# A hybrid attention block on one core: group B by chunks of 64 queries, and the input projection in three turns

## The reference, cut to what matters

```python
proj = x @ w_in                      # 2048 tokens, 1024 -> 2756 columns
qa, ka, va, ga, qi, ki, wi, qb, kb, vb, gb = split(proj)
# group A: 8 heads, one key/value head
score = sum_h wi[h] * relu(qi[h] @ ki.T)          # 4 index heads
idx   = top_k(score where chunk(key) <= chunk(query), 256)
ya    = softmax(qa @ ka[idx].T / 8 - slope * |t - idx|) @ va[idx]
# group B: 8 heads, 2 key/value heads; a chunk of 64 queries
# sees the 64 keys before it and its own 64 keys
yb    = softmax([qb @ kb.T / 8 - slope * dist, sink])[..., :-1] @ vb
y     = concat(ya * silu(ga), yb * silu(gb)) @ w_out
out   = layer_norm(2**0.25 * x + y)
```

## Time and profile before

| | us |
|---|---|
| median of 3 runs (1501.98 to 1502.45) | 1502.32 |
| span of the profiled execution, first to last instruction | 1501.2 |
| PE busy | 1395.7 (93%) |
| DVE busy | 1164.6 (78%) |
| ACT busy | 969.1 (65%) |
| POOL busy | 491.5 (33%) |
| projection, first to last matmul of L1314 | 11.5 to 578 |
| last stage, from its first matmul | from 1316.6 |

### The profile page before, as it was taken

How to read it: one execution, slowest core, us unless ns; L and a number is a source line. 1 busy time by engine, 2 the same in 40 slices (tenths; PEclk the granted TensorE clock), 3 DMA queues, 4 the chain that set the end, 5 groups by cost and what they waited for, 6 DMA issues and landing times. The chain is left out here.

```text
span 1501.2 us, 19745 instructions
## 1 busy us (share of the span) xinstructions
PE 1395.7 (93%) x6551; PEld 1038.2 (69%) x6604; DVE 1164.6 (78%) x2406; ACT 969.1 (65%) x1879; POOL 491.5 (33%) x310
## 2 busy tenths in 40 slices
PE   6998999899999896799899899999998999999997
PEld 5887877678788675556466566566665776578886
DVE  3377879868999888689989998989987756347765
ACT  3385876874789258988549789569997767711010
POOL 1332132651523343412411212112214745423332
PEclk9999999999999997899999999999999999999999
DMA  6322131532222336422211323103214222124442
GB/s 247 98 74 103 57 112 68 165 103 70 90 79 67 129 86 166 98 72 68 72 43 56 77 50 91 55 14 86 67 49 132 85 58 80 43 92 158 150 135 90
DMA packets 104534, 136.42 MB, mean 91 GB/s; under 512 B 6611, under 2 KB 81367, under 8 KB 104175
## 3 DMA queue, kind: packets, MB, share of 16 engines
q1 hardware_dynamic: 91280, 92.73, 22.6%
q10 hardware_dynamic: 9504, 31.66, 5.3%
q0 software_dynamic: 3648, 10.76, 2.3%
HBM read 92.73 MB, written 42.34 MB: 90 GB/s over the span
## 5 line engine op out<-in xcount | busy, mean ns | idle before, releaser
L1612 DVE TENSOR_SCALAR_CACHE_REDUCE above<-dist,trial 128x512 bf16<-128x512 int32 (+13 forms) x224 | 345.5, 1543 | 5.8
L1139 ACT ACTIVATE above<-dist,trial 128x384 bf16<-128x384 int32 (+13 forms) x224 | 280.7, 1253 | 21.5 <-DVE trial L1585 11.7
L1314 PE MATMUL psum<-x_hi,w_hi 128*128 128x512 f32 x640 | 254.6, 398 | 33.3 <-POOL w_lo L941 13.5
L1314 PE MATMUL psum<-x_lo,w_hi 128*128 128x512 f32 x640 | 252.5, 394 | 0.0
L1314 PE MATMUL psum<-x_hi,w_lo 128*128 128x512 f32 x640 | 252.1, 394 | 0.0
L1248 ACT ACTIVATE prob<-psum 128x512 f32<-128x512 f32 x272 | 159.0, 592 | 116.8 <-PE psum L1462 59.0
L1712 DVE CUSTOM_DVE_ANT_0 junk<-psum,mask 128x512 bf16<-128x512 f32 (+3 forms) x320 | 183.1, 605 | 38.9 <-PE psum L1385 19.5
L1462 PE MATMUL psum<-prob,vw 128*65 128x512 f32 x376 | 184.1, 592 | 0.1
L1449 PE MATMUL psum<-qa_mix,ka_mix 128*128 128x512 f32 x272 | 161.5, 594 | 6.3 <-DMA qa_ext<-minus_max 6.1
L1314 PEld LDWEIGHTS psum<-x_hi,w_hi 128*128 128x128 f32 x640 | 122.3, 191 | 62.9 <-POOL w_lo L941 15.7
L933 POOL CAST w_hi<-raw 128x1024 fp32r<-128x1024 f32 x40 | 52.0, 1299 | 286.5 <-PE psum L1314 279.7
(11 more groups left out here) (160 smaller groups left out, 3001.1 us busy)
## 6 DMA issues: line engine op xcount, KB each, us to landing
raw<-w_tiles SPq DMA_DIRECT2D x40, 512.0 KB, 3.8
proj<-staged ACTq DMA_DIRECT2D x40, 512.0 KB, 3.1
qb_raw<-proj SPq DMA_DIRECT2D x32, 256.0 KB, 4.0
qa_raw<-proj SPq DMA_DIRECT2D x32, 256.0 KB, 4.5
yt_raw<-y_t SPq DMA_DIRECT2D x16, 512.0 KB, 5.2
x_row<-x_res SPq DMA_DIRECT2D x16, 512.0 KB, 3.9
out<-z ACTq DMA_DIRECT2D x16, 512.0 KB, 2.6
x_raw<-xT SPq DMA_DIRECT2D x12, 512.0 KB, 4.2
```

The lines of the kernel that those rows point to most:

```text
L1139: nc.scalar.activation(above[:, 0, 0:n], src, ACT.Sign, scale=-1.0, bias=u, accum_out=count[:, 0:1]).then_inc(sign_counted, 1)
L1314: last = pe.matmul(psum[:, 2 * u + m, :], wt[:, u, k, :], xt[:, k, 512 * m:512 * m + 512], start=(k == 0 and q == 0), stop=(k == KT - 1 an ...
L1612: v.tensor_scalar(above[:, 1, 0:n], src, u, None, ALU.is_ge, ALU.add, accum_out=count[:, 1:2]).then_inc(own_counted, 1)
```

## The change

Group B takes chunks of 64 queries: a stationary operand of 128 columns is 64 queries of two heads, the moving operand the 128 keys that this chunk sees. Rows of `lb` are then 128 keys and one sink; no key is masked away. The probabilities are divided by their sum on POOL before they are transposed (`level_b`, new), 8 transposes are enough, and `mix_b` has the values as the stationary operand and 256 columns of probabilities as the moving one, four times. Its result has the rows that the output wants, so `y_b` and `columns_b` are gone. The columns of `w_in` and the rows of `w_out` of group B are permuted on the host for it, and `shift_values` copies the values once, shifted by 64 tokens, into `vs`.

The projection has three turns: tiles 0 to 2 of the first half, all 20 of the second, then tiles 3 to 19 of the first. The first half's x is loaded, rounded and split a second time for the third turn. The splits of the second turn are DVE's (`OWN_SPLITS`), those of the third POOL's. The 16 `norm` steps are bound to the first two turns, and `dots` of steps 1 to 5 stand in the list of the second.

The planner breaks ties in a fixed way, some assumed durations are larger (a search step 0.1 on DVE and 0.08 on ACT), and the table `PREFER` is new throughout.

```diff
+PASSES = [(0, range(0, KEY_TILES - 1)), (1, range(0, N_TILES)), (0, range(KEY_TILES - 1, N_TILES))]
+SEQUENCE = [(half, t) for half, some in PASSES for t in some]
+PLACE = {tile: n for n, tile in enumerate(SEQUENCE)}
+OWN_SPLITS = 2 * KT + 2
...
-            add("DVE", 0.6 + n / 960, "search", p, i, needs=[("begin" if i < 16 else "turn", p), ("search", p, i - 1)])
-            add("ACT", 1.0 + (n - P) * 0.00083, "sign", p, i,
+            add("DVE", 0.7 + n / 960, "search", p, i, needs=[("begin" if i < 16 else "turn", p), ("search", p, i - 1)])
+            add("ACT", 1.08 + (n - P) * 0.00083, "sign", p, i,
...
+        if t == PASSES[turn][1][-1] and turn < 2 and k == 0:
+            needs += [("product", *tiles[n - 1], KT - 1)] + [("norm", b) for b in NORM_ORDER[8 * turn:8 * turn + 8]]
...
-        for p in ((1, 2, 3), (4, 5))[half]:
+        for p in ((), (1, 2, 3, 4, 5), ())[turn]:
             dots_of(p, None)
...
-        add("DVE", 0.2, "den_b", b, needs=[("exp_b", b, H - 1), ("y_b", b - 1)])
+        add("DVE", 0.2, "den_b", b, needs=[("exp_b", b, H - 1), ("level_b", b - 1)])
+        add("POOL", 2.6, "level_b", b, needs=[("den_b", b)])
...
+            def shift_values():
+                sp.wait_ge(tile_mm, 2 * N_TILES)
+                sp.wait_ge(norm_out, NB)
+                sp.dma_start(vs[0:HD, 1:NB, :], vw[HD:P, 0:NB - 1, HD + 1:HD + 1 + P]).then_inc(values_shifted, 16)
+                sp.dma_start(vs[HD:P, :, :], vw[0:HD, :, HD + 1:HD + 1 + P]).then_inc(values_shifted, 16)
...
+            def level_b(b):
+                pool.wait_ge(b_rec, b + 1)
+                settled()
+                nc.gpsimd.tensor_tensor(lb[:, :, 0:P], lb[:, :, 0:P], rec_b[:, :].unsqueeze(2).broadcast_to([P, H, P]),
+                                        ALU.mult).then_inc(b_level, 1)
...
-                pe.wait_ge(b_exp, 2 * b + g + 1)
+                pe.wait_ge(b_level, b + 1)
                 banks_free(2)
-                for i in range(4):
-                    last = pe.transpose(psum[:, 2, P * i:P * i + P], lb[:, 4 * g + i, P:2 * P], ident[:, :])
-                    if b:
-                        last = pe.transpose(psum[:, 3, P * i:P * i + P], lb[:, 4 * g + i, 0:P], ident[:, :])
+                for i in range(H):
+                    last = pe.transpose(psum[:, 2 + i // 4, P * (i % 4):P * (i % 4) + P], lb[:, i, 0:P], ident[:, :])
...
-                for h in range(H):
-                    o = psum[:, 2, HD * h:HD * h + HD]
-                    v0 = HD + 1 + HD * (h // 4)
-                    qs = slice(P * (h % 4), P * (h % 4) + P)
-                    if b:
-                        pe.matmul(o, ptb[:, h // 4, 1, qs], vw[:, BLOCKS[b] - 1, v0:v0 + HD], start=True, stop=False)
-                    last = pe.matmul(o, ptb[:, h // 4, 0, qs], vw[:, BLOCKS[b], v0:v0 + HD], start=(b == 0), stop=True)
+                for g in range(2):
+                    for c in range(2):
+                        keys = vw[:, BLOCKS[b], HD + 1:HD + 1 + P] if c else vs[:, BLOCKS[b], :]
+                        last = pe.matmul(psum[:, 2 + g, 2 * P * c:2 * P * c + 2 * P], keys, ptb[:, g, 2 * P * c:2 * P * c + 2 * P],
+                                         start=True, stop=True)
```

More of the change, by code:

```diff
@@ L84 @@
           "search": ("sortable", "begin", "search", "sign", "turn", "limits", "equal", "above", "masks"),
-          "band": ("load_qb", "round_qb", "split_qb", "window", "bias_b", "max_b", "exp_b", "put_sink", "den_b", "turn_b",
-                   "copy_b", "mix_b", "y_b", "columns_b", "gate_b"),
+          "band": ("load_qb", "round_qb", "split_qb", "window", "bias_b", "max_b", "exp_b", "put_sink", "den_b", "level_b", "turn_b",
+                   "copy_b", "mix_b", "gate_b"),
           "scan": ("load_qa", "round_qa", "split_qa", "positions", "scan", "scan_max", "top_of_chunks", "turn_max", "leave_max", "place_max"),
@@ L141, in timed @@
                 by_engine.setdefault(self.engine[piece], []).append((piece, time))
-            for engine, some in by_engine.items():
+            for engine in ("SP", "POOL", "DVE", "ACT", "PE"):
+                some = by_engine.get(engine, [])
                 now = free.get(engine, 0.0)
@@ L178, in timed, with whole_plan @@
         return start
-def whole_plan(final=True):
+def whole_plan():
     plan = Plan()
     add = plan.add
-    tiles = [(half, t) for half in range(2) for t in range(N_TILES)]
-    x_of = lambda half, k: k + half * (KT + 2)
+    tiles = SEQUENCE
+    x_of = lambda turn, k: k + (KT * turn + 2 if turn else 0)
+    split_kind = lambda m: "split_x" if m < OWN_SPLITS else "split_x2"
     def dots_of(p, bank_lock):
@@ L285, in whole_plan @@
         for k in range(KT):
-            for t in range(2):
-                products(half, t, k)
-        for t in range(2, N_TILES):
+            for t in some[0:2]:
+                products(turn, half, t, k)
+        for t in some[2:]:
             tile(half, t)
-            if (half, t) == (0, N_TILES - 1):
-                for b in NORM_ORDER[0:8]:
+            if t == some[-1] and turn < 2:
+                for b in NORM_ORDER[8 * turn:8 * turn + 8]:
                     norm(b)
             for k in range(KT):
-                products(half, t, k)
@@ L295, in whole_plan @@
-        if half:
-            for b in NORM_ORDER[8:]:
-                norm(b)
-        for p in ((1, 2, 3), (4, 5))[half]:
+                products(turn, half, t, k)
+        for p in ((), (1, 2, 3, 4, 5), ())[turn]:
             dots_of(p, None)
-    end = ("product", 1, N_TILES - 1, KT - 1)
+    end = ("product", *tiles[-1], KT - 1)
     for i in range(2):
-        add("POOL", 1.0, "keys_rest", i, needs=[("norm", NORM_ORDER[-1]), ("split_x2", 2 * KT + 1), ("round_keys", 1)])
+        add("POOL", 1.0, "keys_rest", i, needs=[("norm", NORM_ORDER[-1]), ("round_keys", 0), ("round_keys", 1)])
@@ L1303, in product @@
             def product(half, t, k):
-                g, u = half * N_TILES + t, t % 2
+                g = PLACE[half, t]
+                u = g % 2
+                turn = [turn for turn, (of, some) in enumerate(PASSES) if of == half and t in some][0]
                 if k == 0:
```

338 lines of the change are left out of this document (170 added, 168 removed).

## The result

The changed kernel takes **1513.05 us** (median of 4 runs, 1511.44 to 1513.54) where the kernel before takes 1502.31 beside it: a ratio of 1.0066, 95% interval 1.0053 to 1.0078. It is slower by 0.7%, where I had forecast 1443 and a range of 1410 to 1478.

The account below looks back on a forecast made before the run. PE, busy 93%, was taken as the bound on average, sharing 612 to 900 us with DVE. 1501.2 - 47 (group B) - 12 (order) = 1442 us span; the runs' median lies 1.1 us higher, so 1443, range 1410 to 1478.

Parts of the forecast that it names:

- Group B on PE: Narrower products and fewer transposes in group B's blocks save 3.1 us a block, 47 us of PE's time in all.
- My mark, PE's busy time: Sign set beforehand: PE's busy time should be about 47 us less, plus what the clock gives.
- I count no change of PE's losses there: Attention, 612 to 900 us: the new order's extra DVE work stands against 14 us saved on DVE, so 0.
- a microsecond counts in full from 900 us on: Attention after 900 us: PE idles little, so each microsecond taken from its work shortens the span by as much.
- My own sign: Forecast wrong if PE's idle time from the projection's end to 900 us grows by more than 10 us.
- The order: Projection: the new list wins back 12 of PE's 29 us idle; bounds 29 us won and 10 us lost.
- The third turn: Projection: extra loads, roundings and splits of x cost PE 0, bounded by 3 us; 13 us more before the search.
- The second account, by DVE: Whole kernel counted by DVE's work: last masks at 1177 us, then the work behind them, giving 1470 us.
- DVE is the bound: Rival: the last two blocks wait for the last mask, 1470 us; chance 0.28 shared with the lost half.
- Group B's time is off the path: Rival: only about half of 47 us comes and the order brings nothing, 1477 us; chance within the shared 0.28.
- The chain through POOL stalls PE: Rival: `level_b` waits in POOL's queue and holds up `turn_b` on PE, 1506 us; chance 0.05.
- The contention rule: POOL beside two-SBUF-input DVE instructions may take 6.53 us, not 2.40; for `level_b` in the attention 2.49 was kept.

Follow-up runs that it names:

- before_less_b: The kernel before, order untouched, with half of group B's transposes and mix products left out: 1491.22 us, ratio 0.9921.
- apart: The changed kernel with the planner's list taking one whole weight tile after the other, not alternating between two: 1502.59 us, ratio 0.9994.
- before_tuned: The kernel before with one whole weight tile after the other and a new planner table `PREFER`: 1511.94 us, ratio 1.0070.

## Why the prediction was wrong, step by step

- **Group B on PE, 47 us: right.** The ledger shows 47.2 us less work, the four products start 0.43 us apart, no transpose of an output follows them. My mark, PE's busy time, was a poor one: it fell by 23 us, because the slow clock stretches it.
- **"I count no change of PE's losses there": the step that failed.** I took PE's saved time in the attention off the span one for one, and held the losses of 600 to 900 us for DVE's. `before_less_b` shows the price in the old order: 0.36 us for each microsecond of group B taken away, against 0.86 for each added to the changed kernel. My sentence that a microsecond counts in full from 900 us on came from PE's small idle time there. That idle time was small while the narrow matmuls were there: with half of them left out it went from 11.8 to 23.0 us from 900 us on. By this price the 47 us were worth 17 (10 to 21), and the attention became 11.6 us shorter. My own sign said so too: PE's idle time from the end of the projection to 900 us was 43.7 us before and 57.4 after, 13.7 more where I had set 10 as the mark of being wrong.
- **The order, 12 us won in the projection: wrong, 21 us lost** (13.2 idle, 7.5 slow), beyond my bounds, which ended at 10 lost. The marks that I set said so: the last product at 600 and not near 566, the waits for weight splits at 26.7 and not under 13 us. I compared the table's effect on DVE's search steps and did not read how PE's tiles stand to POOL's splits: alternating, as before, but with no `norm` left as filler between the pairs of the last turn, since all 16 now stand in the first turn and at the start of the second. `apart` puts the price at 38 us of projection. Both steps together make up the miss: 35 us that did not come in the attention, and a projection 22 us longer in place of 12 shorter, against 70 us between 1443 and 1513.
- **The third turn, 0: right**, and in part by luck: products waited 4.4 us for POOL's x splits (I set a mark of 6), and with lists made for each, three turns and two differ by 0.5 us. What it costs at the start was under-counted: the first search began 24 us later, where I had 13, and nothing came of it.
- **The second account, by DVE:** masks foreseen at 1177, seen at 1223, with the tail right (104 for 103.8). It took 189 us for the last stage, which is the stretch from 1312 in the earlier trace rows; the stage begins at 1316.6 and lasts 184.6, so the account gives 1466 and not 1470. Yet DVE was not the bound: 36 to 50 us less of its work moved the masks by under 2 us. The account was nearer to the truth for the wrong reason.
- **The rivals.** *DVE is the bound*: out, by the cuts of its search steps and scans. *Group B's time is off the path*: this is what happened in the attention (1477 was its time; the projection's 21 us lay on top). *The chain through POOL stalls PE*: the sign was right, the mechanism not: PE waited 1.3 us for `level_b` in all, and cutting it down gained 1 us. I gave slower 0.05, and all of it to this mechanism; a worse list had no rival of its own, though the whole table was new.
- **The contention rule.** I kept 2.49 us for `level_b`, and it took 1.90, at most 2.06: in the attention the rule did not bite. In the projection it did, on both engines. DVE's index sums of 512 columns took 1013 ns on average (869 before), POOL's roundings up to 5.02 us.

## What to carry to other kernels

Where an engine is busy for over 90% of a stretch, ask what its cheap steps cover before you count their removal in full: cut them out of the old kernel with the order untouched, and see how much of the time goes. An order that alternates between two tiles leaves the next tile's preparation only the end of the pair; a whole tile after the other gives it a tile's length. Here that was worth 38 us of projection where nothing else stood between the pairs, and some 10 where other matmuls did (`before_tuned`, with a new table). A fixed distance between a step and the end is no proof of a bound as long as nobody has moved the step.

## What the runs showed of the hardware

**POOL and DVE wait for the end of each other's instruction.** An index sum that reads two SBUF tensors takes 0.75 us; this one began 0.04 us ahead of a POOL split of 2.39, took 2.98, and ended 0.55 us after the split. POOL's rounding, one tensor in and one out, takes 1.04 us; this one began 2.3 us after a DVE instruction of 6.45 us on two tensors, took 5.02, and ended 0.90 us after it. DVE, then POOL, then DVE and POOL (in order of time):

```profile
371.07 2.98 DVE L1571 SCALAR_TENSOR_TENSOR score<-relu,vw,score 128x512 f32<-128x512 f32 x1
```

```profile
371.11 2.39 POOL L955 TENSOR_TENSOR x_lo<-x_raw,x_hi 128x1024 fp32r<-128x1024 f32 x1 [2.70 <-ACT x_hi L1104]
```

```profile
404.60 6.45 DVE L1586 TENSOR_TENSOR score<-score,dist 128x4096 int32<-128x4096 int32 x1
```

```profile
406.93 5.02 POOL L938 CAST w_hi<-raw 128x1024 fp32r<-128x1024 f32 x1 [0.16 <-POOL w_lo L946]
```

The chain of the longest wait above has the same pattern three times. The split from 533.81 ended at 540.08, 2.1 us after the second scan on DVE (537.95). DVE's instruction from 537.98 ended at 544.36, 4.3 us after that split. The rounding from 540.24 ended at 545.26, 0.9 us after it. So the wait is what is left of the other engine's instruction: 4.1 us each for the split and for this rounding. The Trainium skill (Trainium Architecture — The Big Picture, What this means for kernel authors) calls the port that DVE and GpSimd share an exclusive lock, not a split of bandwidth; these rows agree. Not every pair collides: a search step (one tensor, 2.35 us) from 456.69 and a rounding (1.05) from 457.28 both took their usual time. A split that moves from POOL to DVE, or a mask that falls beside a weight split, is to be priced with the wait.

**Idle time is paid again in clock.** Over the two kernels 34 us more of idle time came with 24 us more of slow clock; in `before_less_b` 17 came with 8.0. It is no fixed rate: `before_tuned` has 3 us more of idle time in the attention than the kernel before and 11.5 more of slow clock. Between the end of the projection and the last stage the slow part was 32% of the idle time before and 45% after.
